# PEER expert blocks with ready hidden values: from the first twenty pairs to every third pair; where the gelu's result lies; which queue loads the spreading stage's tables

## The reference, cut to what matters

```python
hid = jnp.einsum('td,thkd->thk', xb, u_tab[ib]).astype(F32)
hid = jax.nn.gelu(hid, approximate=False) * gb
return jnp.einsum('thk,thkd->td', hid.astype(xb.dtype), v_tab[ib])
```

## Time and profile before

| | us |
|---|---|
| median of 3 runs | 2727.41 |
| the profiled execution | 2733.32 |
| its span | 2731.8 |
| TensorE busy, share of the span | 87% |
| VectorE busy | 66% |
| ScalarE busy | 28% |
| GpSimd busy | 29% |

### The profile page before, as it was taken

The page is one execution under the profiler, slowest core; times in us unless marked ns, Lnnn a source line. Parts: engine busy times, 40 slices in busy tenths (PEclk is TensorE's granted clock), DMA queues, the critical chain, the costliest instruction groups (busy, mean ns, idle before and its releaser), DMA issues. The chain is left out here.

```text
span 2731.8 us, 44652 instructions
## 1 busy us (share of the span) xinstructions
PE 2374.5 (87%) x16971; PEld 2064.9 (76%) x16971; DVE 1815.9 (66%) x3598; ACT 756.5 (28%) x1264; POOL 804.7 (29%) x619
## 2 busy tenths in 40 slices
PE   2999888698879887999878758999999999999998
PEld 2899777575524786776556638999888899999998
DVE  2661555544484534999477616668999978888887
ACT  1322111122321310122356522333222232323231
POOL 2000000000022000333100018866656655656562
PEclk8999898896578898999988869999999999999999
DMA  2233000222074412223255567777777767777771
GB/s 66 70 94 106 7 3 3 61 71 95 16 254 162 140 47 72 68 67 118 81 137 134 152 204 277 257 257 265 270 279 288 287 223 271 261 265 260 260 273 60
DMA packets 253437, 428.95 MB, mean 157 GB/s; under 512 B 81029, under 2 KB 183872, under 8 KB 238561
## 3 DMA queue, kind: packets, MB, share of 16 engines
q1 hardware_dynamic: 211041, 275.80, 31.4%
q0 software_dynamic: 42240, 151.03, 15.4%
HBM read 383.10 MB, written 43.68 MB: 156 GB/s over the span
## 5 line engine op out<-in xcount | busy, mean ns | idle before, releaser
L2456 PE MATMUL experts_pV<-experts_GH,experts_VH 128*128 128x392 f32 x1024 | 370.4, 362 | 40.9 <-POOL experts_GL L2539 19.9
L2543 POOL TENSOR_TENSOR experts_VL<-experts_V,experts_VH 128x2048 fp32r<-128x2048 f32 x64 | 295.3, 4614 | 355.2 <-ACT experts_VH L2489 354.0
L2456 PE MATMUL experts_pV<-experts_GH,experts_VL 128*128 128x392 f32 x1024 | 349.9, 342 | 0.0
L2456 PE MATMUL experts_pV<-experts_GL,experts_VH 128*128 128x392 f32 x1024 | 349.8, 342 | 0.0
L2589 DVE TENSOR_TENSOR keep_xT<-experts_pV,keep_xT 128x392 f32<-128x392 f32 x512 | 277.3, 556 | 64.1 <-PE experts_pV L2456 63.7
L2585 DVE TENSOR_TENSOR experts_G<-experts_G,experts_M 128x392 f32<-128x392 f32 x88 | 209.6, 2382 | 124.2 <-ACT experts_G L2495 124.2
L2445 PE MATMUL experts_pH<-keep_xh,experts_UH 128*128 128x392 f32 x704 | 242.1, 344 | 0.4
L2445 PE MATMUL experts_pH<-keep_xl,experts_UH 128*128 128x392 f32 x704 | 239.9, 341 | 0.0
L2445 PE MATMUL experts_pH<-keep_xh,experts_UL 128*128 128x392 f32 x704 | 239.3, 340 | 0.0
L2456 PEld LDWEIGHTS experts_pV<-experts_GH,experts_VH 128*128 128x128 f32 x1024 | 193.7, 189 | 55.8 <-issue 41.1
L2456 PEld LDWEIGHTS experts_pV<-experts_GL,experts_VH 128*128 128x128 f32 x1024 | 194.3, 190 | 0.0
(11 more groups left out here) (431 smaller groups left out, 5200.3 us busy)
## 6 DMA issues: line engine op xcount, KB each, us to landing
experts_V<-in_peer_v SPq DMA_DIRECT2D x64, 1024.0 KB, 6.6
experts_U<-in_peer_u SPq DMA_DIRECT2D x44, 1024.0 KB, 8.5
scratch_gates<-spread_M SPq DMA_DIRECT2D x3, 7680.0 KB, 31.8
experts_M<-scratch_gates SPq DMA_DIRECT2D x64, 360.0 KB
keep_K<-in_cache_k SPq DMA_DIRECT2D x64, 256.0 KB, 3.5
keep_V<-in_cache_v POOLq DMA_DIRECT2D x64, 256.0 KB, 4.0
front_w<-in_w_in SPq DMA_DIRECT2D x30, 512.0 KB, 3.8
pick_U<-in_peer_u SPq DMA_DIRECT2D x24, 512.0 KB, 3.8
```

Of the source, the lines that this page charges most:

```text
L2456: last = nc.tensor.matmul(pV[n % 4][:, 0:DT], l, r, start=(t == 0), stop=(t == 5))
L2543: nc.gpsimd.tensor_tensor(VL[q.b][:, :, :], V[q.b][:, :, :], VH[q.b][:, :, :].bitcast(F32), ALU.subtract).then_inc(v_lo, 1)
```

## The change

1. In the spread stage, the tables of U and the finished hidden values are issued by GpSimd's queue; SyncE's queue keeps the four stores of the gate table.
2. The stages pick and spread store U x without the gelu (`clear` with Copy in the place of `gelu`).
3. In the experts, pairs 4, 7, 10, ... 61 (20 of them) are V-only; pairs 0 to 3 are full. The loop has six pairs a pass and makes 5 passes, twice. Before the first step TensorE now does U x of pair 0 and turns pair 1. GpSimd issues its first ten gathers before the first `rest_v`.
4. The gelu of every pair, an early one too, is made in the experts, and its result goes to the PSUM bank `pH`; `gate` reads it there and writes `G`. So `gelu` waits no more for `g_lo`, `gate` does, and `product_u` waits for `gated` in place of `gelued`.
5. The rows used by a pair are spread anew: five parts for a step whose pair q is full, one where it is early.

```diff
 # spread, SyncE and GpSimd
-            table(0)
-            table(1)
-            for u in range(NU):
-                n, k = divmod(u, STEPS)
-                if k == STEPS - 1 and n < SPREAD_BLOCKS:
-                    if n + 2 < NB:
-                        table(n + 2)
-                    keep(n)
-                if u in last_of:
-                    store(last_of[u])
-            for n in range(SPREAD_BLOCKS, NB):
+        @blk.gpsimd
+        def _(pool):
...
+            table(0)
+            table(1)
+            for n in range(NB):
                 if n + 2 < NB:
                     table(n + 2)
                 keep(n)
...
-                sc(nc)(hid[n % 2][:, :], pH[n % 2][:, 0:DT], ACT.Gelu).then_inc(gelued, 1)
+                sc(nc)(hid[n % 2][:, :], pH[n % 2][:, 0:DT], ACT.Copy).then_inc(cleared, 1)
 # experts
+    PERIOD = 6
+    TURN = 2 + 5 * PERIOD
...
+                self.early = off >= 4 and off % 3 == 1
...
+        def share(n):
+            return 0 if n == TURN else 1 if Pair(n + 1).early else 5
 
         def until(n):
+            lo, hi, k = (0, TURN, 0) if n <= TURN else (TURN + 1, NB, K)
+            return k + sum(share(m) for m in range(lo, n)) * K // sum(share(m) for m in range(lo, hi))
...
-                if q.after(NE + 1):
-                    pe.wait_ge(gelued, q.ucount(2, e - 1))
+                if q.after(1):
+                    pe.wait_ge(gated, q.count(2, e - 1))
...
+            def first():
+                for st in range(4):
+                    turn(pe, Pair(0), st)
+                product_u(pe, Pair(0))
+                for st in range(4):
+                    turn(pe, Pair(1), st)
...
         def gelu(act, q, e):
-            act.wait_ge(hidden, q.ucount(2, e + 1))
-            if q.after(1):
-                act.wait_ge(g_lo, q.count(2, e - 1))
-            sc(nc)(G[e][:, :], pH[e][:, 0:DT], ACT.Gelu).then_inc(gelued, 1)
+            if q.early:
+                act.wait_ge(u_in[q.b], q.loads())
+                act.wait_ge(gated, q.count(2, e - 1))
+                sc(nc)(pH[e][:, 0:DT], U[q.b][:, e, 0:DT], ACT.Gelu).then_inc(gelued, 1)
+            else:
+                act.wait_ge(hidden, q.ucount(2, e + 1))
+                sc(nc)(pH[e][:, 0:DT], pH[e][:, 0:DT], ACT.Gelu).then_inc(gelued, 1)
...
-            all_of(Pair(0))
             for n in range(SLOTS):
                 gather(pool, n)
+            all_of(Pair(0))
...
-            nc.vector.tensor_tensor(G[e][:, :], made, M[q.b][:, e, :], ALU.mult).then_inc(gated, 1)
+            dve.wait_ge(gelued, q.count(2, e + 1))
+            if q.after(1):
+                dve.wait_ge(g_lo, q.count(2, e - 1))
+            nc.vector.tensor_tensor(G[e][:, :], pH[e][:, 0:DT], M[q.b][:, e, :], ALU.mult).then_inc(gated, 1)
```

More of the change, by code:

```diff
@@ L1914, in peer_choose @@
         loaded, done, u_in, kept = ([s.sem(f"{n}{e}") for e in range(2)] for n in ("loaded", "done", "u_in", "kept"))
-        queried, u_turned, cut, hidden, gelued = (s.sem(n) for n in ("queried", "u_turned", "cut", "hidden", "gelued"))
+        queried, u_turned, cut, hidden, cleared = (s.sem(n) for n in ("queried", "u_turned", "cut", "hidden", "cleared"))
         blk = s.block()
@@ L2054, in _ @@
                         cut_table(n + 1)
-                    gelu(n)
+                    clear(n)
             act.wait_ge(shifted, 1)
@@ L2192, in _ @@
         def _(sp):
[L2193 to L2203, removed]
+            for n, (t0, w) in enumerate(SPREAD):
                 sp.wait_ge(out, 2 * ((t0 + w) // TB))
@@ L2361, in __init__, with at @@
                 self.off, self.i, self.b = off, i, off % 2
+                self.early = off >= 4 and off % 3 == 1
+                self.nth = (off - 4) // 3 if self.early else off - max(0, (off - 2) // 3)
+            def at(self, n, step):
+                return n if self.i is None else self.i * step + n
             def count(self, per, n):
-                return per * self.off + n if self.i is None else self.i * (2 * per) + (per * self.off + n)
+                return self.at(per * self.off + n, per * PERIOD)
@@ L2367, in loads, with ucount, blocks @@
+            def ucount(self, per, n):
+                assert not self.early
+                return self.at(per * self.nth + n, per * (PERIOD - 2))
             def loads(self, each=1):
                 n = 16 * each
-                return n * (self.off // 2 + 1) if self.i is None else self.i * n + n * (self.off // 2 + 1)
-            def ucount(self, per, n):
-                return self.count(per, n - per * NE)
+                return self.at(n * (self.off // 2 + 1), n * (PERIOD // 2))
+            def blocks(self):
+                if self.early:
+                    return bass.ds(self.at(2 * self.nth, 2 * 2), 2)
+                return bass.ds(self.at(EARLY + 2 * self.nth, 2 * (PERIOD - 2)), 2)
@@ L2376, in after, with uafter, before @@
             def after(self, n):
                 return self.i is not None or self.off >= n
+            def uafter(self, n):
+                return self.i is not None or self.nth >= n
+            def before(self, n):
+                return Pair(self.off - n, self.i)
         def schedule(eng, first, body, tail, between=None):
             first()
-            for p in range(NE):
-                body(Pair(p), Pair(p + 1), Pair(p + 2))
-            for lo, hi in ((NE // 2, TURN // 2), (TURN // 2, NQ // 2 - 1)):
+            for m in range(2):
+                body(Pair(m), Pair(m + 1), Pair(m + 2))
@@ L2386, in schedule @@
+            for lo, hi in ((0, 5), (5, 10)):
                 with eng.Fori(lo, hi) as i:
-                    for off in range(2):
+                    for off in range(2, 2 + PERIOD):
                         body(Pair(off, i), Pair(off + 1, i), Pair(off + 2, i))
-                if hi == TURN // 2 and between:
+                if lo == 0 and between:
                     between()
             tail()
-        def early(q):
-            return q.i is None and q.off < NE
+        def share(n):
+            return 0 if n == TURN else 1 if Pair(n + 1).early else 5
@@ L2411, in load @@
-            if early(q):
+            at = q.blocks()
+            if q.after(2):
+                old = q.before(2)
+                if old.early:
+                    sp.wait_ge(gelued, old.count(2, 2))
+                else:
+                    sp.wait_ge(turned, old.ucount(4, 4))
+            if q.early:
                 sp.dma_start(U[k][:, :, 0:DT], hscr[:, at, :]).then_inc(u_in[k], 16)
@@ L2610, in _ @@
             nc.vector.memset(ys[:, :], 0.0)
+            for st in range(4):
+                rest_u(dve, Pair(0), st)
             for e in range(2):
                 gate(dve, Pair(0), e)
+            for st in range(4):
+                rest_u(dve, Pair(1), st)
             for m in range(NB):
@@ L2618, in _ @@
                 for n in range(ND):
-                    if n % 2 == 0 and not early(r):
+                    if n % 2 == 0 and not r.early:
                         rest_u(dve, r, n // 2)
```

75 lines of the change are left out of this document (34 added, 41 removed).

## The result

The changed kernel takes 2647.12 us in the median of 4 runs (2643.97 to 2648.26), the kernel before on the same chip 2732.36: a ratio of 0.969, with an interval of 0.9656 to 0.9725. Run again later, beside experiments 10 to 12, it had 2650.64 us and 0.971 (0.9696 to 0.9725). The prediction said 2645. The profiled execution took 2648.13 us, 85.2 less than the one of before. 60.6 of them fell between VectorE's first instruction of the spread stage and the start of the split (264.4 us before, 203.9 after), 20.0 between the first load of the experts and the first transpose of the store (1100.7 and 1080.7), and 4.5 ahead of the spread stage. That last part isn't a gain that can be put down to the change: in the profiles of this document the spread stage begins anywhere from 1338.5 to 1348.5 us.

The account below looks back on a forecast made before the run. VectorE and TensorE bound the spread units, TensorE nearly all the experts. Gains of 60 us there and 26 in the experts (100 over floors to 44 + 9 + 21 = 74) made 86: forecast 2645, range 2605 to 2700.

Parts of the forecast that it names:

- The queue: Spread stage: tables leave SyncE's queue, so TensorE's waits behind stores go; 60 us gained, from 45 to 66.
- The delay of 0.5 us for each issue: Spread stage: GpSimd's descriptors delay VectorE by some 0.5 us for each of 32 issues; used for the lower end.
- Gates at 0.55 us: Experts: a gate with one SBUF input takes an add's 0.55 us, against 2,382 ns.
- The wait of an early pair: Experts: TensorE waits in V-only steps for late VectorE work; 2.2 us each, 44 us for 20, from 0 to 4.5 each.
- The 9 us for all other steps: Experts: the 44 other steps lose 0.2 us each over their floor, 9 us.
- The start: Start of the experts: TensorE's loss is 21 us instead of 25, from 15 to 30.
- the loops' excess, 61 us: Experts before: full pairs over their floors, 40 us in 16 of the first loop and 21 in 26 of the second.
- the 14 of the V-only pairs: Experts before: V-only pairs take 9.27 us each, 0.72 over the floor, 14 us in 20.
- the long loop: Rival: TensorE's six-pair loop needs instruction fetches at eight jumps back, 55 us, total 2700; chance 0.07.
- Rows beside all of `rest_v`: Slower rival, experts: late `rest_v` makes rows meet its 4.61 us; up to 92 us, total 2737 to 2829; chance 0.07.
- the gathers hold GpSimd: Argument against the slow rival: gathers end with the rows, so `rest_v` ends before C's (r early) first row at 11.3 us.
- no wait remains: Rival, experts: no wait in the early pair, the 44 us and half the rest also gained, about 2600; chance 0.16.

Follow-up runs that it names:

- experiments 10 to 12: 10: kernel before with queue and PSUM gate, 2628.82 us; 11: the same with gathers three rows later, 2694.84 us; 12: changed kernel without rows, 2581.35 us.
- experiment 11: Kernel before with the new queue and the gate in PSUM, old order of pairs, gathers issued three rows later: 2694.84 us, ratio 0.987.
- experiment 12: Changed kernel without the rows and their gathers, so the last 128 tokens get nothing from the experts: 2581.35 us, ratio 0.9453.
- the two parts in the old order: Kernel before with only the spread stage's tables on GpSimd's queue and full pairs' gelu kept in PSUM for the gate: 2628.82 us, ratio 0.9631.
- experiment 8: Changed kernel with an early pair's gelus first on ScalarE, and rows before it moved behind the first adds, none behind the last: 2627.92 us.
- run 9: The changed kernel itself, run again on another chip: 2650.64 us, ratio 0.971.
- run 6: Changed kernel with both gelus of an early pair at the head of ScalarE's step, ahead of the cuts: 2639.75 us, ratio 0.9672.

## Why the prediction was right, and where only in its sum

- **The queue: right**, 60 predicted, 60.6 in the profile and 61 alone. The tables landed within 9.6 us. The delay of 0.5 us for each issue, which I had put on VectorE for the lower end, doesn't show: a block of units takes 13.29 us before and after. The Trainium skill, SBUF — State Buffer, section Who interferes with whom, would have kept GpSimd from writing its descriptors while VectorE runs a mode with both port pairs. The trace shows nothing of that: each table was issued in 0.53 to 0.58 us, with VectorE busy 160.8 of the 166.4 us of the units. Whether VectorE was in such a mode there, no run tells. For the same section's other statement, that an instruction of VectorE with two inputs in SBUF shuts out one of GpSimd that reads SBUF, and the other way round, experiment 11 is a clear case: 1.04 us for two gates apart from `rest_v`, 5.40 beside it.
- **Gates at 0.55 us: right** (0.563). What it is worth was not reckoned by itself: 38 us alone.
- **The wait of an early pair: right in place, cause and size, but not in what follows it.** I put 2.2 us on a pair, up to 2.7 in the second half, for the chain of late rows, gate, `cut_g`, gelu, gate, low part: 44 us. TensorE waited 15.6 us in the 10 periods of the first half, 20.6 in the 8 of the second and 7.3 in the last, 43.5 in all. The 9 us for all other steps didn't come (0.7 us of waits for adds). What the term left out is the work behind a wait: the same instructions keep TensorE busy 6.1 and 15.0 us longer in the two halves than without rows. Two and six falls of the granted clock to 0.50, at some 1.7 us each, make 13.6 of these 21 us; where the other 7 come from isn't shown. So the periods' excess is 69 us, not 44 + 9: 23 and 37 in the two halves, and 9 from the last early pair on, where a row took 6.05 us (from that pair's cut of V to the store 64.9 us, and 55.7 without rows).
- **The start: mis-sized.** The floors of all pairs are 44 x 18.81 + 20 x 8.55 = 998.6 us. The experts took 1080.7, so 82.1 over, and without the 69 some 13 are left for the start, where I said 21, from 15 to 30.
- So the experts gained 20 us, not 26: 16 too little on the periods, 8 too much on the start, and 2 more over the floors before than I had counted (1100.7 - 998.6 = 102). That the whole came out so near is luck: the 6 us that the experts fell short are about the 4.5 by which the spread stage began sooner, which I hadn't forecast.
- **What the sum hid.** I priced the gate and the order together, from 100 us over the floors to 74. Apart they have opposite signs: the gate gains 38, the rest costs 22. The step of the reckoning that failed is that I let all of the loops' excess, 61 us, go with the new order. In the old order the gate alone takes 39 of it (21.33 to 20.09 in 16 pairs, 19.61 to 18.89 in 26). So the order removes only the other 22 and the 14 of the V-only pairs, and adds 69; with 12 us that the start has gained (25 to 13) it loses 21, and 22 were measured.
- **Rivals.** No pass of six pairs begins with a wait of TensorE, and in experiment 12 the same loop leaves TensorE no pause at all, so the long loop cost nothing. Rows beside all of `rest_v` came once: the row of 6.05 us, when the gathers were over and GpSimd ran ahead; TensorE waited 7.3 us, the longest of all. Three rows of 4.6 us met the last 1.6 us of a `rest_v`, and `rest_g`. Else the gathers hold GpSimd, as I had argued. That no wait remains came true only without rows.

Two kernels here are as fast as each other and faster than the changed one: the two parts in the old order (2628.82 us beside 2650.64) and the new order with both edits of experiment 8 (2627.92 us).

## What to carry to other kernels

A change of several parts is priced part by part, each against the kernel before: here a part that costs 22 us lay hidden under two that gain 61 and 38. Work that isn't on the critical path, like these rows, is put where the engine that sets the pace still has a long product ahead of it, and not in front of a step that has none. And a wait that keeps two instructions apart can be worth more than its removal: look at what the freed engine will meet.

## What the runs showed of the hardware

- A wait of TensorE of some 2 us can cost more than its length, in clock. Behind the start of the experts the changed kernel waited 19 times for a low part. After none of the 7 waits of 1.20 to 1.55 us did the granted clock fall; after 9 of the 12 of 2.18 to 7.30 us it was 0.50 for some 3 us, after three (2.24, 2.40 and 2.51 us) it stayed at 1.00. A period of the second half with a wait of 2.40 us and no fall took 49.2 us, one with 2.54 us and a fall 51.0. In the second profile of this kernel (run 9) it fell after 11 of 12 such waits, and in run 6 once after a wait of 1.75 us. With both edits (run 8) no wait in the loops is longer than 2.0 us, and the clock never fell there.
- A gather's issue on GpSimd that begins while a row runs on VectorE takes 1.3 to 2.0 us (89 of 99 in the changed kernel). One that begins ahead of a row takes 0.94 us, though the row starts within it, and one beside no row 0.94. Rows take 1.2 to 1.3 us alone, and up to 7 us where they meet `rest_g` or `rest_v`.
- Three stores of 7.5 MB on a queue of their own land in 35.6 us each in the median. The eight tables of 512 KB that GpSimd's queue issues beside them land in 5.1 to 9.6 us, the other eight in 3.8 to 4.9.
